# Reordering the down stage of a seven-product FFN unit in a two-layer decoder kernel

## The chip, the core and the metric

The kernel is one program on one core of a Trainium2 chip. Times are device microseconds (us) from the first to the last work of the core; the number compared is the median over several executions. The profile is of one execution, taken by the hardware profiler. TensorE multiplies matrices, VectorE (DVE) and ScalarE (ACT) work elementwise, GpSimd (POOL) does small things, SyncE (SP) issues the weight loads. PE in the rows is TensorE, PEld its weight load.

## The reference, cut to what matters

Two layers; each is an attention and pooling part, then a gated FFN with a causal three-tap convolution, then a gated per-layer embedding. The change lies in the FFN and in the stage behind it.

```python
D_MODEL = 2048; SEQ = 256; DEPTH = 2; D_FF = 5632; PLE_DIM = 256

def conv_gated_ffn(x, w_up, conv_w, conv_b, w_down):
    gu = x @ w_up                                   # (256, 2048) @ (2048, 11264)
    gate, up = gu[..., :D_FF], gu[..., D_FF:]
    gate = causal_depthwise_conv(gate, conv_w, conv_b)
    return (jax.nn.silu(gate) * up) @ w_down        # (256, 5632) @ (5632, 2048)

for i in range(DEPTH):
    ...
    h = h + conv_gated_ffn(rms_norm(h, norm_ffn_g[i]), w_up[i], conv_w[i], conv_b[i], w_down[i])
    gate = jax.nn.sigmoid(rms_norm(h, norm_ple_g[i]) @ w_ple_gate[i])
    h = h + (p[i] @ w_ple[i]) * gate
```

All of it is float32. The kernel gets that accuracy from TensorE by splitting every operand x into hi (x rounded to the fast format) and lo = x - hi, and by adding three products: hi*hi, lo*hi and hi*lo.

## The kernel before, in words

**Halves.** Weights arrive in chunks of 128 x 2048 numbers in four buffers (`raw`), loaded by SP. A chunk has two halves of 128 x 1024. ACT copies a half to `w_hi` (L989), then DVE subtracts it from the raw half into `w_lo` (L1551); I call the latter a split. There are six buffers of each kind for halves, so ACT can write half n only when TensorE has used half n-6. ACT and DVE work four halves ahead of their place in the program (`go(a, b)` splits halves a+4 to b+4-1). SP loads a chunk into a raw buffer once the last split that reads the old chunk is done (L537 to 545).

**Units.** The 5632 channels of the FFN are 11 units of 512. `first_unit` computes gate and up of unit 0. Then a loop of five rounds, two units in each, does ten times: gate (8 halves, numbers 0 to 7) and up (8 to 15) of unit u, then down of unit u-1. Behind the loop down of the last unit is done by four plain blocks (L2413). In all there are 20 loop units in the two layers.

**Down.** The product of 256 tokens x 512 channels with 512 x 2048 weights is cut by columns into four blocks of 512. Two of them are plain: two halves each, 24 matmuls per half. The other two are done together by a Strassen-like form with seven block products instead of eight: seven halves of 12 matmuls each. These are B11, B21, B22, T1, T3, T2, T4 (`corner_product`, L2341); the T weights are differences of quarters, which DVE forms in place in `raw` (`t_sum`, L1559, four subtractions of 128 x 1024). In the kernel before the seven are halves 16 to 22 and the plain blocks are halves 23 to 26, so a unit has 27 halves.

**Results.** A product lands in a PSUM bank: `acc` is two pairs of banks, `tps` four banks. DVE adds it to `h` (`by_token`, L1520) or to one of four kept sums in `corner_sum` (L1680), and the add frees the bank: it counts up `acc_free[0]`, `acc_free[1]` or `t_done`. TensorE waits for that count before it writes the bank again (`free_acc`, L1908, `new_job`, L1933). Gate of the next unit starts in `acc[0]`, so its first matmul waits for the last add out of `acc[0]`. The kept sums are combined once per layer, in `fold` (L1748), before the last unit's block is added to `h`.

**Order.** Each engine's order of work is written out by hand. There is no scheduler; an engine waits at its next instruction until its counts are there. What stands in which order on DVE in the down stage is L1714 to 1741.

Of the kernel before, what the change touches and what calls it, by code (L numbers as in the profile page):

```python
# [27 lines left out]
P = 128  # L28
# [99 lines left out]
def build(nc, x, p, positions, norm_mix_g, w_in, pool_w, pool_scale, q_norm_g, w_uq, kv_norm_g, w_ukv,  # L128
# [56 lines left out]
    with ExitStack() as ctx:  # L185
# [25 lines left out]
        with ExitStack() as early:  # L211
            sb("below_corners", [P, KT // 2, S], scope=early)
            corner_sum = sb("corner_sum", [P, 4, BLK], scope=early)
# [5 lines left out]
        mask = sb("mask", [P, 2 * P])  # L219
        win = sb("win", [P, 2, 2, PAD + S])  # L220
# [46 lines left out]
        with ExitStack() as scope:  # L267
# [4 lines left out]
            sb("below_p", [P, 3, S], scope=scope)  # L272
# [97 lines left out]

        LAT_Q, LAT_KV = 0, LKT
# [25 lines left out]
        def chunk_of(m):  # L397
# [3 lines left out]
        FORM_B11, FORM_B21, FORM_B22, FORM_T1, FORM_T3, FORM_T2, FORM_T4 = range(2 * 2 * (KT // 4), 2 * 2 * (KT // 4) + CORNERS)  # L401
        PLAIN = FORM_T4 + 1
        IN_RAW = {FORM_B11: (0, 0), FORM_B21: (0, 1), FORM_B22: (1, 1), FORM_T1: (0, 0), FORM_T3: (1, 0),
                  FORM_T2: (1, 1), FORM_T4: (0, 1)}

        def raw_half(n):

            down = 2 * (KT // 4)
            if n >= UNIT_HALVES:
                return UNIT_CHUNKS + (n - UNIT_HALVES) // 2, n - UNIT_HALVES & 1  # L410
            if n >= PLAIN:
                return down + 2 + (n - PLAIN) // 2, (n - PLAIN) & 1
            if n >= FORM_B11:
                return down + IN_RAW[n][0], IN_RAW[n][1]
            return n // 2, n & 1
# [19 lines left out]
        def _(sp):  # L435
            def load(l, c, pieces):
# [4 lines left out]
                if 0 <= c - (CH["ple"] - N_BLK) < 2:  # L441
                    m = 2 * RAW_SLOTS + M_DOWN - UNIT_HALVES + FORM_T4 + 1
# [48 lines left out]
            for l in range(L):  # L491
# [45 lines left out]
                def load_at(l, w, i, n, pieces):  # L537
                    slot = (c + n) % RAW_SLOTS
                    first = M_UNIT + i * UNIT_HALVES + 2 * RAW_SLOTS
                    freed = (-(UNIT_HALVES - 1 - FORM_T4),) * 2 + (-2, 0) if n < RAW_SLOTS else [2 * (n - RAW_SLOTS) + 2]  # L540
                    sp.wait_ge(lo_done, HALVES * l + LOOP_HALVES * w + first + freed[n if n < RAW_SLOTS else 0])
# [43 lines left out]
        def _(pool):  # L585
# [60 lines left out]
            for l in range(L):  # L646
# [12 lines left out]
                pool.memset(corner_sum[:, :, :], 0.0).then_inc(corners_zero, 1)  # L659
# [35 lines left out]
        def _(act):  # L695
# [88 lines left out]
            for l in range(L):  # L784
# [194 lines left out]
                def split_u(l, w, i, n):  # L979
# [6 lines left out]
                    if FORM_T1 <= n <= FORM_T4:  # L986
                        act.wait_ge(t_made, made(l, w, i, n - FORM_T1 + 1))
# [152 lines left out]
        def _(dve):  # L1140
# [18 lines left out]
            dve.memset(win[:, :, :, 0:PAD], 0.0)  # L1159
# [88 lines left out]
            for l in range(L):  # L1248
# [75 lines left out]
                def pooled(i):  # L1324
                    u = u_pool[i][:, :, PAD:PAD + S]
                    dve.memset(u_pool[i][:, :, 0:PAD], 0.0)
                    for k in range(2):
# [226 lines left out]
                def corner(i, k, half):  # L1554

                    slot = (CH["ffn"] + 4 * (KT // 4) + i * UNIT_CHUNKS + k) % RAW_SLOTS
                    return raw[:, slot, half * HALF:(half + 1) * HALF]

                def t_sum(w, i, k, dst, a, b):  # L1559

                    if k == 1:
                        c = CH["ffn"] + 4 * (KT // 4) + i * UNIT_CHUNKS + 1
# [104 lines left out]
                def unit(w, i):  # L1667
# [834 lines left out]
```

## Time and profile before

| what | value |
|---|---|
| median of 3 runs | 2183.87 us (2181.57, 2183.87, 2183.98) |
| the profiled execution: its time, its span | 2181.74 us, 2179.9 us |
| granted TensorE clock, mean | 0.998 of full |
| busy: PE, PEld, DVE, ACT, POOL | 99%, 85%, 79%, 51%, 2% of the span |
| chain that ended last | PE 92%, DVE 4%, issue 3% |
| DMA | 406.75 MB, mean 187 GB/s |

The table is read from the top: TensorE is busy nearly all the time, so the time is its work plus its few idle stretches. The other engines' shares are means over stages; what counts is whether one of them is late where TensorE waits for it. The slices of the span show TensorE at 9 tenths or more in all but the last, and VectorE at 8 tenths in the FFN.

### The profile page before, as it was taken

How to read it: one execution, taken by the hardware profiler on the slowest of the kernel's cores; microseconds unless marked ns; L12 is line 12 of the kernel's file. 1: busy time of each engine (PE TensorE's matmuls, PEld its weight loads, DVE VectorE, ACT ScalarE, POOL GpSimd, SP SyncE). 2: the span in 40 equal slices, each digit the busy share in tenths (PEclk: the TensorE clock that was granted, in tenths of full speed). 3: DMA queues.
4: the chain of work that ended last, by engine and by line, in shares of the span. 5: the costliest groups of instructions: out<-in, count | busy, mean ns of one | idle time of the engine just before them, and what ended most of it. 6: DMA issues, size and time to landing. Idle time of an engine off the chain costs nothing.

```text
span 2179.9 us, 32733 instructions
## 1 busy us (share of the span) xinstructions
PE 2149.6 (99%) x11526; PEld 1858.8 (85%) x11526; DVE 1730.0 (79%) x2213; ACT 1119.1 (51%) x1419; POOL 48.9 (2%) x112
## 2 busy tenths in 40 slices
PE   9999999999999999999999999999999999999998
PEld 8898888888888888878898988888888888888786
DVE  6797569888889888896557975789888889888964
ACT  6555545544455544545554654455554555554554
POOL 2000000000000000000000000000000000000011
PEclk9999999999999999999999999999999999999999
DMA  7745555446655446645556455555546655446462
GB/s 265 213 136 175 187 196 199 170 154 217 213 195 198 170 154 224 212 174 188 176 185 175 136 192 170 203 194 189 178 154 230 212 193 193 168 159 231 174 213 97
DMA packets 233323, 406.75 MB, mean 187 GB/s; under 512 B 14828, under 2 KB 50268, under 8 KB 233096
## 3 DMA queue, kind: packets, MB, share of 16 engines
q1 hardware_dynamic: 231976, 402.72, 54.8%
q0 software_dynamic: 512, 1.76, 0.2%
q8 instruction: 48, 0.79, 0.1%
q10 hardware_dynamic: 736, 1.07, 0.1%
q14 instruction: 51, 0.42, 0.1%
HBM read 403.42 MB, written 2.10 MB: 186 GB/s over the span
## 4 chain that ended last, share of the span: by engine, by line
PE 92%; DVE 4%; issue 3%; ACT 0%; DVEq 0%; POOL 0%; POOLq 0%; ACTq 0%
PE acc L2078 16%; PE tps L2078 16%; PE acc L1897 12%; PE acc L1899 12%; PE acc L1898 11%; PE tps L2088 8%; PE acc L2088 8%; DVE w_lo L1551 2%; PE tps L1898 2%; PE tps L1899 2%; PE tps L1897 2%; PE tps L1954 1%; PE acc L1984 1%; DVE h L1521 1%; DVE corner_sum L1680 1%
## 5 line engine op out<-in xcount | busy, mean ns | idle before, releaser
L989 ACT ACTIVATE w_hi<-raw 128x1024 fp32r<-128x1024 f32 x540 | 556.8, 1057 | 554.7 <-PE acc L2088 116.6
L1551 DVE TENSOR_TENSOR w_lo<-raw,w_hi 128x1024 fp32r<-128x1024 f32 x540 | 649.4, 1224 | 158.0 <-ACT w_hi L989 145.5
L1175 DVE TENSOR_TENSOR w_lo<-raw,w_hi 128x1024 fp32r<-128x1024 f32 (+1 forms) x288 | 342.4, 1211 | 144.4 <-ACT w_hi L715 138.7
L715 ACT ACTIVATE w_hi<-raw 128x1024 fp32r<-128x1024 f32 (+2 forms) x287 | 290.2, 1043 | 179.3 <-PE acc L1899 127.0
L2078 PE MATMUL acc<-xa,w_hi 128*128 128x512 f32 x1536 | 366.1, 391 | 0.0
L2078 PE MATMUL tps<-xa,w_hi 128*128 128x512 f32 x1536 | 361.2, 390 | 0.0
L2078 PEld LDWEIGHTS tps<-xa,w_hi 128*128 128x128 f32 x1536 | 285.5, 188 | 57.1
L2078 PEld LDWEIGHTS acc<-xa,w_hi 128*128 128x128 f32 x1536 | 283.9, 188 | 56.0 <-DVE h L1513 0.4
L1898 PE MATMUL acc<-w_hi,xb_lo 128*128 128x512 f32 x640 | 249.3, 390 | 0.0
L1897 PE MATMUL acc<-w_hi,xb_hi 128*128 128x512 f32 x560 | 220.8, 394 | 0.0
L1899 PE MATMUL acc<-w_lo,xb_hi 128*128 128x512 f32 x560 | 218.4, 390 | 0.0
L2088 PEld LDWEIGHTS acc<-xa,w_lo 128*128 128x128 f32 x1536 | 192.8, 192 | 5.1
L2088 PE MATMUL acc<-xa,w_lo 128*128 128x256 f32 x1536 | 194.3, 283 | 0.0
L2088 PEld LDWEIGHTS tps<-xa,w_lo 128*128 128x128 f32 x1536 | 190.7, 192 | 3.7
L2088 PE MATMUL tps<-xa,w_lo 128*128 128x256 f32 x1536 | 191.8, 283 | 0.0
L1898 PEld LDWEIGHTS acc<-w_hi,xb_lo 128*128 128x128 f32 x640 | 120.4, 188 | 23.9
L1899 PEld LDWEIGHTS acc<-w_lo,xb_hi 128*128 128x128 f32 x560 | 105.2, 188 | 22.0
L1897 PEld LDWEIGHTS acc<-w_hi,xb_hi 128*128 128x128 f32 x560 | 105.3, 188 | 20.7
L1897 PE MATMUL acc<-w_hi,gt_hi 128*128 128x512 f32 x240 | 95.7, 399 | 9.2 <-DVE w_lo L1551 9.2
L1567 DVE TENSOR_TENSOR raw<-raw 128x1024 f32<-128x1024 f32 x80 | 97.6, 1220 | 0.0
L1898 PE MATMUL acc<-w_hi,gt_lo 128*128 128x512 f32 x240 | 93.7, 390 | 0.0
L1899 PE MATMUL acc<-w_lo,gt_hi 128*128 128x512 f32 x240 | 93.6, 390 | 0.0
(263 smaller groups left out, 2676.3 us busy)
## 6 DMA issues: line engine op xcount, KB each, us to landing
raw<-in_w_up SPq DMA_DIRECT2D x176, 1024.0 KB, 5.0
raw<-in_w_down SPq DMA_DIRECT2D x88, 1024.0 KB, 5.0
raw<-in_w_out SPq DMA_DIRECT2D x32, 1024.0 KB, 5.0
raw<-in_w_ple_gate SPq DMA_DIRECT2D x32, 1024.0 KB, 5.0
raw<-in_w_in SPq DMA_DIRECT2D x21, 1024.0 KB, 5.4
raw<-in_w_ukv SPq DMA_DIRECT2D x8, 1024.0 KB, 5.6
raw<-in_w_in SPq DMA_DIRECT2D x8, 864.0 KB, 4.8
raw<-in_w_uq SPq DMA_DIRECT2D x6, 1024.0 KB, 5.6
```

Of the source, the lines that this page charges most:

```text
L715: copy(w_hi[:, half_of(m), 0:n], raw[:, c % RAW_SLOTS, at:at + n], ACT.Copy).then_inc(hi_done, 1)
L989: copy(w_hi[:, half_of(m), :], raw[:, c % RAW_SLOTS, half * HALF:(half + 1) * HALF], ACT.Copy).then_inc(hi_done, 1)
L1175: dve.tensor_tensor(w_lo[:, half_of(m), 0:n], raw[:, c % RAW_SLOTS, at:at + n], w_hi[:, half_of(m), 0:n].bitcast(F32), ALU.subtract).then_ ...
L1521: return dve.scalar_tensor_tensor(dst, src, rstd["ffn"][:, t:t + 1], dst, ALU.mult, ALU.add)
L1551: dve.tensor_tensor(w_lo[:, half_of(m), :], raw[:, slot, half * HALF:(half + 1) * HALF], w_hi[:, half_of(m), :].bitcast(F32), ALU.subtract ...
L1567: dve.tensor_tensor(dst, a, b, ALU.subtract).then_inc(t_made, 1)
L1680: ins = dve.tensor_tensor(dst, src, dst, ALU.add)
L1897: pe.matmul(dst, a_hi, b_hi, start=first, stop=False)
L1898: pe.matmul(dst, a_lo, b_hi, start=False, stop=False)
L1899: return pe.matmul(dst, a_hi, b_lo, start=False, stop=last)
L2078: ins = pe.matmul(dst, hi[:, k * BLK + n * P:k * BLK + (n + 1) * P], x_both[:, kt, :, :].rearrange("p a s -> p (a s)"), start=kt == 0, sto ...
L2088: ins = pe.matmul(bank(n, False)[:, S:2 * S], lo[:, k * BLK + n * P:k * BLK + (n + 1) * P], xa[0][:, kt, :], start=False, stop=False)
```

## The change

The order of the down stage is changed on all engines. Halves 16 and 17 are B11 and B21, then comes a plain block (18, 19), then B22 and T1 (20, 21), then the other plain block (22, 23), then T3, T2 and T4 (24 to 26). The plain blocks are now column blocks 0 and 1, the seven-product blocks 2 and 3. The seven products' weights come from chunks 10 and 11 of a unit instead of 8 and 9, the plain ones from 8 and 9. The banks move with it: the first plain block is in `acc[1]`, B22 and T1 in `tps` 0 and 1, the second plain block in `tps` 2 and 3, T3 in `acc[0]`, T2 and T4 in `tps` 0 and 1. The four subtractions for the T weights stand later on DVE. `fold` works at blocks 2 and 3 of the last unit. The kept sums are in `corner_3` and `corner_4`, cleared by two instructions on POOL; one clearing of `win` on DVE moves from the start into each layer.

```diff
@@ the numbers of the halves
-        FORM_B11, FORM_B21, FORM_B22, FORM_T1, FORM_T3, FORM_T2, FORM_T4 = range(2 * 2 * (KT // 4), 2 * 2 * (KT // 4) + CORNERS)
-        PLAIN = FORM_T4 + 1
+        DOWN = 4 * (KT // 4)
+        FORM_B11, FORM_B21, PLAIN_0, _, FORM_B22, FORM_T1, PLAIN_1, _, FORM_T3, FORM_T2, FORM_T4 = range(
+            DOWN, DOWN + N_BLK + CORNERS)
...
+        LAST_LO = (PLAIN_0 + 1, PLAIN_1 + 1, FORM_T4, FORM_T4)
@@ loads, SP
-                    freed = (-(UNIT_HALVES - 1 - FORM_T4),) * 2 + (-2, 0) if n < RAW_SLOTS else [2 * (n - RAW_SLOTS) + 2]
+                    if n < RAW_SLOTS:
+                        freed = max(LAST_LO[n] + 1 - UNIT_HALVES, 2 * (n + 1) - 2 * RAW_SLOTS)
+                    else:
+                        freed = 2 * (n - RAW_SLOTS) + 2
@@ one unit, DVE
                     tap_1(u)
                     go(12, 13)
                     tap_0(u)
+                    go(13, 15)
+                    silu(u)
+                    go(15, 16)
                     t_sum(w, i, 1, corner(i, 0, 0), corner(i, 1, 0), corner(i, 0, 0))
-                    go(13, 15)
+                    go(16, 17)
                     t_sum(w, i, 2, corner(i, 1, 0), corner(i, 1, 1), corner(i, 1, 0))
-                    silu(u)
+                    gated(u)
+                    go(17, 18)
                     t_sum(w, i, 3, corner(i, 1, 1), corner(i, 1, 1), corner(i, 0, 0))
-                    go(15, 16)
+                    go(18, 20)
+                    dve.wait_ge(corners_zero, 2 * l + 2)
+                    product_added(FORM_B11, sum_p1, acc[0][:, 0, :], None, acc_free[0])
+                    product_added(FORM_B21, h_block(0, 2), acc[0][:, 1, :], 0, acc_free[0])
                     t_sum(w, i, 4, corner(i, 0, 1), corner(i, 0, 1), corner(i, 1, 1))
-                    go(16, 17)
-                    gated(u)
-                    go(17, 19)
-                    dve.wait_ge(corners_zero, l + 1)
-                    product_added(FORM_B11, corner_sum[:, 0], acc[0][:, 0, :], None, acc_free[0])
-                    product_added(FORM_B21, h_block(0, 0), acc[0][:, 1, :], 0, acc_free[0])
-                    go(19, 21)
-                    product_added(FORM_B22, h_block(0, 1), acc[1][:, 0, :], 0, acc_free[1])
-                    product_added(FORM_T1, corner_sum[:, 1], acc[1][:, 1, :], None, acc_free[1], 3)
-                    go(21, 22)
-                    product_added(FORM_T3, corner_sum[:, 2], tps[:, 0, :], None, t_done)
-                    product_added(FORM_T2, corner_sum[:, 3], tps[:, 1, :], None, t_done)
-                    go(22, 23)
-                    product_added(FORM_T4, h_block(1, 0), tps[:, 2, :], 1, t_done)
-                    go(23, 25)
-                    for t in range(TT):
-                        product_added(PLAIN + 1, h_block(t, 2), acc[0][:, t, :], t, acc_free[0])
-                    go(25, 27)
-                    for t in range(TT):
-                        product_added(PLAIN + 3, h_block(t, 3), tps[:, (3 + t) % T_BANKS, :], t, t_done, 1 if t == 0 else 4)
+                    go(20, 22)
+                    product_added(PLAIN_0 + 1, h_block(0, 0), acc[1][:, 0, :], 0, acc_free[1])
+                    product_added(PLAIN_0 + 1, h_block(1, 0), acc[1][:, 1, :], 1, acc_free[1], 3)
+                    go(22, 24)
+                    product_added(FORM_B22, h_block(0, 3), tps[:, 0, :], 0, t_done)
+                    product_added(FORM_T1, sum_p5, tps[:, 1, :], None, t_done)
+                    go(24, 26)
+                    product_added(PLAIN_1 + 1, h_block(0, 1), tps[:, 2, :], 0, t_done)
+                    product_added(PLAIN_1 + 1, h_block(1, 1), tps[:, 3, :], 1, t_done)
+                    product_added(FORM_T3, sum_p7, acc[0][:, 0, :], None, acc_free[0], 2)
+                    go(26, 27)
+                    product_added(FORM_T2, sum_p6, tps[:, 0, :], None, t_done)
+                    product_added(FORM_T4, h_block(1, 2), tps[:, 1, :], 1, t_done, 3)
@@ the last unit, DVE (fold)
-                    if j >= 2:
+                    if j < 2:
                         return
@@ one unit, TensorE
                     corner_product(m0 + FORM_B11, w, a11, acc[0][:, 0, :])
                     corner_product(m0 + FORM_B21, w, a12, acc[0][:, 1, :])
+                    for _ in down(m0 + PLAIN_0, b0 + 3, gt, w):
+                        pass
                     pe.wait_ge(s_split_lo, (UNITS - 1) * l + u)
-                    free_acc(l, b0 + 3, w)
-                    corner_product(m0 + FORM_B22, w, s4, acc[1][:, 0, :])
-                    corner_product(m0 + FORM_T1, w, s1, acc[1][:, 1, :])
-                    for n, a in ((0, s3), (1, s2), (2, a22)):
-                        corner_product(m0 + FORM_T3 + n, w, a, new_job(l, j0 + 4 + n, w))
-                    for _ in down(m0 + PLAIN, b0 + 4, gt, w):
+                    corner_product(m0 + FORM_B22, w, s4, new_job(l, j0 + 4, w))
+                    corner_product(m0 + FORM_T1, w, s1, new_job(l, j0 + 5, w))
+                    for _ in down(m0 + PLAIN_1, None, gt, w, j0 + 6):
                         pass
-                    for _ in down(m0 + PLAIN + 2, None, gt, w, j0 + 7):
-                        pass
+                    free_acc(l, b0 + 4, w)
+                    corner_product(m0 + FORM_T3, w, s3, acc[0][:, 0, :])
+                    corner_product(m0 + FORM_T2, w, s2, new_job(l, j0 + 8, w))
+                    corner_product(m0 + FORM_T4, w, a22, new_job(l, j0 + 9, w))
```

The end of a unit on DVE before, from the add of T4 on (`w_lo` rows are splits, rows with `rstds` add a product to `h`):

```order
L1521 SCALAR_TENSOR_TENSOR h<-tps,rstds,h 128x512 [waits w_used]
L1551 TENSOR_TENSOR w_lo<-raw,w_hi 128x1024 [waits w_used,hi_done] x2
L395 REGISTER_ALU
L1521 SCALAR_TENSOR_TENSOR h<-acc0,rstds,h 128x512 [waits w_used] x2
L1549 REGISTER_ALU
L1551 TENSOR_TENSOR w_lo<-raw,w_hi 128x1024 [waits w_used,hi_done] x2
L395 REGISTER_ALU
L1521 SCALAR_TENSOR_TENSOR h<-tps,rstds,h 128x512 [waits w_used] x2
```

The same end on DVE in the changed kernel, from the splits of halves 28 and 29 on:

```order
L1556 REGISTER_ALU
L1558 TENSOR_TENSOR w_lo<-raw,w_hi 128x1024 [waits w_used,hi_done]
L1556 REGISTER_ALU
L1558 TENSOR_TENSOR w_lo<-raw,w_hi 128x1024 [waits w_used,hi_done]
L1528 SCALAR_TENSOR_TENSOR h<-tps,rstds,h 128x512 [waits w_used] x2
L396 REGISTER_ALU
L1687 TENSOR_TENSOR corner_3<-acc0,corner_3 128x512 [waits w_used]
L1558 TENSOR_TENSOR w_lo<-raw,w_hi 128x1024 [waits w_used,hi_done]
L396 REGISTER_ALU
L1687 TENSOR_TENSOR corner_3<-tps,corner_3 128x512 [waits w_used]
L396 REGISTER_ALU
L1528 SCALAR_TENSOR_TENSOR h<-tps,rstds,h 128x512 [waits w_used]
```

Before, the last adds out of `acc0` had two splits and two adds behind them. Now the last add out of `acc0` (T3) has one split and two adds behind it, and two splits and two adds of the second plain block directly ahead.

DVE between the last tap of the convolution and the silu before, with the first two subtractions for the T weights (`raw<-raw`):

```order
L1567 TENSOR_TENSOR raw<-raw 128x1024 [waits raw_landed3]
L1549 REGISTER_ALU
L1551 TENSOR_TENSOR w_lo<-raw,w_hi 128x1024 [waits w_used,hi_done]
L1549 REGISTER_ALU
L1551 TENSOR_TENSOR w_lo<-raw,w_hi 128x1024 [waits w_used,hi_done]
L1566 REGISTER_ALU
L1567 TENSOR_TENSOR raw<-raw 128x1024 [waits t_made]
L1616 REGISTER_ALU
L1617 SCALAR_TENSOR_TENSOR conv<-gate_f,conv 128x1024 [waits tanh_done]
```

The same place in the changed kernel:

```order
L1556 REGISTER_ALU
L1558 TENSOR_TENSOR w_lo<-raw,w_hi 128x1024 [waits w_used,hi_done]
L1556 REGISTER_ALU
L1558 TENSOR_TENSOR w_lo<-raw,w_hi 128x1024 [waits w_used,hi_done]
L1623 REGISTER_ALU
L1624 SCALAR_TENSOR_TENSOR conv<-gate_f,conv 128x1024 [waits tanh_done]
L1556 REGISTER_ALU
L1558 TENSOR_TENSOR w_lo<-raw,w_hi 128x1024 [waits w_used,hi_done]
L1570 ISA
L1574 TENSOR_TENSOR raw<-raw 128x1024 [waits raw_landed1]
```

The first subtraction stood directly behind the last tap; now three splits and the silu stand between them.

TensorE at the end of a unit in the changed kernel, T4 and the first matmuls of the next gate:

```order
L1903 MATMUL tps<-w_hi,gt_hi 128x512 [waits lo_done]
L1904 MATMUL tps<-w_hi,gt_lo 128x512
L1905 MATMUL tps<-w_lo,gt_hi 128x512
L1903 MATMUL tps<-w_hi,gt_hi 128x512
L1904 MATMUL tps<-w_hi,gt_lo 128x512
L1905 MATMUL tps<-w_lo,gt_hi 128x512
L1911 REGISTER_ALU
L1919 REGISTER_ALU [waits lo_done]
L2084 MATMUL acc0<-xa,w_hi 128x512 [waits acc_free0]
```

The wait for `acc_free0` ahead of the gate was there before too; what stands ahead of it is now T4 in `tps` and not a plain block.

## Rows read from the trace of the kernel before

**Rows 1.** One loop unit: length, busy time of each engine, PEclk, DMA share, GB/s

```profile
635.10:700.70 65.60, 65.14 (x349) 56.22 (x348) 57.00 (x67) 32.52 (x33) 0.00 (x0) 1.00 0.56 192
```

**Rows 2.** Waits of TensorE, whole span: waiter, releaser: us in total, times, longest

```profile
PE acc L1897 <- DVE w_lo L1551: 9.2, 20, 0.5
PE tps L1954 <- DVEq L1518: 8.6, 4, 2.6
...
PE tps L1954 <- DVE h L1521: 1.2, 2, 0.6
```

**Rows 3.** Timeline of TensorE in that unit: start, us, instruction [idle before, releaser]

```profile
631.35 0.84 PE L2078 MATMUL acc<-xa,w_hi 128*128 128x512 f32 x3
...
675.81 0.39 PE L1897 MATMUL acc<-w_hi,gt_hi 128*128 128x512 f32 x1
...
685.10 0.39 PE L1899 MATMUL tps<-w_lo,gt_hi 128*128 128x512 f32 x1
685.95 0.49 PE L1897 MATMUL acc<-w_hi,gt_hi 128*128 128x512 f32 x1 [0.46 <-DVE w_lo L1551]
...
696.95 3.79 PE L2078 MATMUL acc<-xa,w_hi 128*128 128x512 f32 x16
```

**Rows 4.** Timeline of DVE in the same unit, second half

```profile
667.31 1.22 DVE L1567 TENSOR_TENSOR raw<-raw 128x1024 f32<-128x1024 f32 x1
669.47 2.36 DVE L1551 TENSOR_TENSOR w_lo<-raw,w_hi 128x1024 fp32r<-128x1024 f32 x2 [0.94 <-ACT w_hi L989]
...
681.07 2.35 DVE L1551 TENSOR_TENSOR w_lo<-raw,w_hi 128x1024 fp32r<-128x1024 f32 x2
683.34 0.69 DVE L1680 TENSOR_TENSOR corner_sum<-acc,corner_sum 128x512 f32<-128x512 f32 x1
683.94 0.74 DVE L1521 SCALAR_TENSOR_TENSOR h<-acc,rstds,h 128x512 f32<-128x512 f32 x1
...
694.52 1.41 DVE L1521 SCALAR_TENSOR_TENSOR h<-acc,rstds,h 128x512 f32<-128x512 f32 x2
...
699.43 2.36 DVE L1551 TENSOR_TENSOR w_lo<-raw,w_hi 128x1024 fp32r<-128x1024 f32 x2
```

**Rows 5.** Timeline of ACT in the same unit

```profile
663.08 1.07 ACT L989 ACTIVATE w_hi<-raw 128x1024 fp32r<-128x1024 f32 x1 [2.70 <-PE tps L2078]
...
668.40 3.10 ACT L989 ACTIVATE w_hi<-raw 128x1024 fp32r<-128x1024 f32 x3
674.19 1.07 ACT L989 ACTIVATE w_hi<-raw 128x1024 fp32r<-128x1024 f32 x1 [2.70 <-PE tps L2078]
```

**Rows 6.** The loads of chunks 10 and 11, and all loads' time to landing

```profile
657.92 5.80 SPq L544 DMA_DIRECT2D raw<-in_w_down  x2
...
DMA to landing us min/median/max: 4.8/5.0/7.1
```

**Rows 7.** Timeline of TensorE behind the last unit of layer 0

```profile
979.95 1.09 PE L1954 MATMUL tps<-ident,h 128*128 128x128 f32 x8 [2.62 <-DVEq L1518]
986.36 1.09 PE L1954 MATMUL tps<-ident,h 128*128 128x128 f32 x8
...
996.37 0.48 PE L1897 MATMUL acc<-w_hi,xb_hi 128*128 128x512 f32 x1
```

**Rows 8.** ACT there: the copies that free the banks of the embedding product

```profile
994.94 2.03 ACT L1065 ACTIVATE pw<-acc 128x512 f32<-128x512 f32 x4
```

**Rows 9.** POOL and DVE at the start of the last unit's down, layer 0

```profile
956.77 2.51 POOL L662 TENSOR_TENSOR xa<-conv,xa 128x1024 fp32r<-128x1024 f32 x1 [672.60 <-ACT xa L1042]
...
958.25 3.24 DVE L1551 TENSOR_TENSOR w_lo<-raw,w_hi 128x1024 fp32r<-128x1024 f32 x2
```

**Rows 10.** The same place in layer 1: TensorE, and the granted clock

```profile
2060.64 1.97 PE L1954 MATMUL tps<-ident,h 128*128 128x128 f32 x8 [2.62 <-DVEq L1518]
...
2068.47 1.03 PE L1954 MATMUL tps<-ident,h 128*128 128x128 f32 x8
...
2060.00:2062.00 2.00, 1.36 (x7) 1.36 (x8) 1.75 (x2) 1.38 (x5) 0.00 (x0) 0.55 0.47 180
```

More of the change, by code:

```diff
@@ L219, in build @@
         mask = sb("mask", [P, 2 * P])
+        with ExitStack() as early:
+            corner_3 = sb("corner_3", [P, 3, BLK], scope=early)
         win = sb("win", [P, 2, 2, PAD + S])
@@ L369, in build @@
         t_made = sem("t_made")
+        sum_p1, sum_p7, sum_p6, sum_p5 = corner_3[:, 0], corner_3[:, 1], corner_3[:, 2], corner_4[:, :]
         LAT_Q, LAT_KV = 0, LKT
@@ L399, in chunk_of @@
             return m // 2 if m < M_DOWN else (m - EXTRA) // 2
[L401 to L404 removed]
+        DOWN = 4 * (KT // 4)
+        FORM_B11, FORM_B21, PLAIN_0, _, FORM_B22, FORM_T1, PLAIN_1, _, FORM_T3, FORM_T2, FORM_T4 = range(
+            DOWN, DOWN + N_BLK + CORNERS)
+        IN_RAW = {PLAIN_0: (0, 0), PLAIN_0 + 1: (0, 1), PLAIN_1: (1, 0), PLAIN_1 + 1: (1, 1),
+                  FORM_B11: (2, 0), FORM_B21: (2, 1), FORM_B22: (3, 1), FORM_T1: (2, 0), FORM_T3: (3, 0),
+                  FORM_T2: (3, 1), FORM_T4: (2, 1)}
+        T_ORDER = (FORM_T1, FORM_T3, FORM_T2, FORM_T4)
+        LAST_LO = (PLAIN_0 + 1, PLAIN_1 + 1, FORM_T4, FORM_T4)
         def raw_half(n):
[L408 removed]
             if n >= UNIT_HALVES:
                 return UNIT_CHUNKS + (n - UNIT_HALVES) // 2, n - UNIT_HALVES & 1
[L411 to L414, printed above, removed]
+            if n >= DOWN:
+                return 2 * (KT // 4) + IN_RAW[n][0], IN_RAW[n][1]
             return n // 2, n & 1
@@ L658, in _ @@
                     p_landed, 16)
-                pool.memset(corner_sum[:, :, :], 0.0).then_inc(corners_zero, 1)
+                pool.memset(corner_3[:, :, :], 0.0).then_inc(corners_zero, 1)
+                pool.memset(corner_4[:, :], 0.0).then_inc(corners_zero, 1)
                 pool.wait_ge(g_hi, UNITS * l + UNITS)
@@ L1157, in _ @@
             step(dve.reciprocal(inv_cnt[:, :], inv_cnt[:, :]))
-            dve.memset(win[:, :, :, 0:PAD], 0.0)
             step(dve.memset(k_lo[ROPE:P, 0, :].bitcast(F32), 0.0))
@@ L1326, in pooled @@
                     dve.memset(u_pool[i][:, :, 0:PAD], 0.0)
+                    if i == 0:
+                        dve.memset(win[:, :, :, 0:PAD], 0.0)
                     for k in range(2):
@@ L1748, in fold @@
                 def fold(l, j):
-                    if j >= 2:
+                    if j < 2:
                         return
-                    p1, p5, p7, p6 = (corner_sum[:, k] for k in range(4))
-                    if j == 0:
+                    p1, p5, p7, p6 = sum_p1, sum_p5, sum_p7, sum_p6
+                    if j == 2:
                         dve.wait_ge(acc_free[0], BLOCKS * l + BL["ple"] - N_BLK + 2)
-                        dve.wait_ge(acc_free[1], BLOCKS * l + BL["ple"] - N_BLK)
                         dve.wait_ge(t_done, JOBS * l + JB["p"] + T_BANKS)
-                    done = 8 * l + 4 * j
-                    if j == 0:
+                    done = 8 * l + 4 * (j - 2)
+                    if j == 2:
                         dve.tensor_tensor(p6, p6, p1, ALU.add).then_inc(corner_folded, 1)
-                        by_token(h[:, 0, 0:BLK], p1, 0).then_inc(corner_folded, 1)
+                        by_token(h[:, 0, 2 * BLK:3 * BLK], p1, 0).then_inc(corner_folded, 1)
                         dve.wait_ge(corner_folded, done + 2)
```

26 lines of the change are left out of this document (12 added, 14 removed).

## The prediction

> **What bounds the kernel now.** I read four views in this order: busy time by stretch, waits of TensorE, timelines of one loop unit engine by engine, and the stage behind the last unit. The stretch of one loop unit shows a length of 65.60 us with TensorE busy for 65.14 and DVE for 57.00 [rows 1]. So TensorE sets the length and DVE has 8.6 us to spare, but as a mean over the unit. The waits say where DVE is late all the same: 20 times, once per loop unit, TensorE waits 0.46 us for a split; behind the last unit of a layer it waits for `h` (two waits of 2.62 us, so 1.7 for each of the other two, and two of 0.6) [rows 2].
>
> I count unit time from the first gate matmul at 631.35. The down stage starts at 675.81, which is 44.46. 41 matmuls later, at 685.10, one sees the pace, 9.29 / 41 = 0.2266 us [rows 3]. So a short half (12 matmuls) takes 2.72 / 2 = 1.36 us and a plain half (24) 5.44 / 2 = 2.72 us. All 90 matmuls take 20.40, while the stage took 696.95 - 675.81 = 21.14: the lost time is 0.74 us per unit, around the wait at 685.95 [rows 3]. Twenty of those, 14.8 us, is all that a better order of the down stage could win.
>
> DVE: the splits at 681.07 (two, the next instruction at 683.34) give 1.135 us for an instruction on 128 x 1024; the add at 683.34 gives 0.60 for an add to a kept sum, and two adds in 1.41 us, of which one takes 0.74, give 0.66 for an add to `h` [rows 4]. From 669.47 (unit time 38.12) until the next unit's first splits at 699.43 the DVE rows follow one another with no idle time: 29.96 us, which is 14 splits, three subtractions and the silu (18 x 1.135), 2.5 for the two steps of the gated product, four adds to kept sums and seven to `h`. That stretch is the tight place. Its last instructions run 2.5 us into the next unit, which costs nothing today, because the last add out of `acc[0]` starts at 694.52 and is over at 695.93, a microsecond before the next gate needs that bank at 696.95 [rows 3, 4].
>
> **The change, part by part.** *Order on TensorE.* The same 90 matmuls, so 20.40 us. Start of each half in unit time without waits: B11 44.46, B21 45.82, plain 47.18 and 49.90, B22 52.62, T1 53.98, plain 55.34 and 58.06, T3 60.78, T2 62.14, T4 63.50, end 64.86. The next gate could start at 64.86.
>
> *Splits.* In the new order of DVE, half 23 is split after 17 to 22, the silu, the gated product and three subtractions: 38.12 + 11 x 1.135 + 2.5 = 53.1, against a need at 58.06. Half 26 has, beyond that, one subtraction, three splits and four adds: 53.1 + 4 x 1.135 + 0.60 + 3 x 0.66 = 60.2, against 63.50. So the wait of today goes: -0.74.
>
> *What is late next: the add of T3.* T3 is in `acc[0]`, the bank where the next gate starts, and its add stands on DVE behind the splits of 28 and 29 and both adds of the second plain block. I get its place by difference. The first subtraction moves out of the time before 38.12 into the stretch, so the stretch has 29.96 + 1.135 = 31.10 us. Behind T3's add stand one split, T2's add and T4's: 1.135 + 0.60 + 0.66 = 2.40. T3's add therefore ends (with the 0.09 by which rows overlap) at 38.12 + 28.70 + 0.09 = 66.91. One small idle time comes in: half 20's hi copy ends at 674.19 + 1.07, unit time 43.91 [rows 5], and DVE would be free for its split at 38.12 + 5 x 1.135 = 43.80: 0.11 more. TensorE starts 0.13 after DVE's end (split over at 683.34 + 0.60 + 0.66 + 1.22 = 685.82, matmul at 685.95). The next gate starts at 66.91 + 0.11 + 0.13 = 67.15, not at 64.86: a wait of 2.3 us in place of one of 0.74, so +1.55 us on 65.60.
>
> Does DVE come back into step? It would be done with the unit at 66.9 + 0.1 + 2.3 = 69.3, which is 2.2 us into the next unit (2.5 today), and its splits in the gate stage wait for TensorE's pace as before, so the stretch again starts at 38.12. The start is set by ACT: its copies of halves 17 to 19 start at 668.40 behind the tanh, and the first ends at 669.47 [rows 5]. The subtraction that stands at 667.31 today fills that time; now DVE idles there. Each unit hence takes 67.15. The bank of T2 needs B22's add, due at about 62.3 against 62.14: 0.2 us, swallowed by the longer wait. Twenty times the stage hands over to something that starts in `acc[0]` (18 gates, and twice the last unit's blocks): 20 x 1.55 = +31.0. Bounds: if the idle time of 0.11 doesn't come, 20 x 1.44 = 28.8; if DVE lost one more row of 0.4 us to a hi copy that comes late, 20 x 1.95 = 39. I take 31.0.
>
> *Loads.* Halves 16 and 17 now come from chunk 10, which is issued at 657.92 and lands in 5.0 us at the median, 662.9; ACT wants it at 663.08 [rows 5, 6]. Cost 0, by 0.2 us of margin; at the longest landing seen, 7.1, it would be 1.9 late, of which DVE, still in its taps then, hides about 0.4. Chunk 11 is wanted 10 us after it lands, and the next gate's first two chunks are issued earlier than today: 0.
>
> *Behind the last unit.* Folds at blocks 0 and 1 are gone: the waits of 1.7 and 2.6 fall away, and so does the 0.6 (T2's add is over by 68.7, TensorE wants its bank at 67.15 + 2.72). With no fold TensorE runs from one transposition to the next without a wait, 979.95 to 986.36 [rows 7]. The fold at block 2 brings a wait of 2.6 back. The one at block 3 is hidden from the transpositions, but it delays ACT's copies that free the embedding product's banks: today the first two are over at 994.94 + 1.0, and TensorE starts in that bank at 996.37 [rows 7, 8], so of 2.7 us of fold 2.3 come out as a wait. Removed 4.9, added 4.9 per layer: 0, between -2.3 (if the copies aren't what waits) and +0.4.
>
> *POOL at the last unit.* Its subtraction takes 2.51 us, and beside it two splits took 3.24 instead of 2.36 [rows 9]. In the new order ACT frees it at about 64.4, so it ends at about 67.0, just when TensorE may start: 0 to 1.0 per layer; I take 0.5, +1.0 in all. The Trainium skill, page "SBUF — State Buffer", section "SBUF: two separate sides", has an exclusive lock there between GpSimd and a VectorE instruction with two SBUF inputs; the rows agree in that one side is held up, and by the lock POOL would start only after the split of 29, some 0.6 later.
>
> *The rest.* Clearing the sums in two pieces is hidden in POOL's 98% of idle time; the clearing of `win` stands where DVE waits for ACT; 0.
>
> Sum: 31.0 + 0 + 1.0 = +32.0 on the profiled execution's 2181.74 (its span and 1.8 us around it): 2213.7. Two of the three runs shown stand 2.2 us above it, so the median would be nearer 2216; I say 2215.
>
> **The rivals.** *A. The clock falls in the new waits.* In layer 1 a wait of 2.62 us was followed by a granted clock of 0.55 over two microseconds, a mix of 2.4 GHz and 1.2 GHz, and the way to the next transpositions took 2068.47 - 2060.64 = 7.83 us against 6.41 in layer 0 after the same wait, which did not lower it [rows 7, 10]: 1.4 us. The new wait of 2.3 lies between that and the waits of 1.7, after which nothing fell. If it fell after half of them: 2215 + 14 = 2229, after all of them 2243. Against: the full clock in layer 0, and the work before and after is dense. The Trainium skill, page "TensorE: Matmul & The Clock Gate", section "A second HAM failure mode: psum-queue depth-cycling", says that frequent short idles between groups of matmuls let the clock go to and fro; by that rule the time is this rival's. The trace agrees only in part, since 20 waits of 0.46 left the clock at full.
>
> *B. Faster: DVE catches up, and the new order pays.* T3's add would have to end by 64.86 - 0.13 = 64.7, which is 2.3 us, two splits, earlier. It would, if DVE's stretch began right behind the last tap at 667.31 (35.96) instead of waiting for ACT until 38.12, or if instructions were shorter in their new places. Then the 0.74 is won 20 times: 2167. Against: the wait for the hi copy behind the tanh is in every unit, and no row of the stretch has any idle time to give.
>
> *C. The add is late by only 0.6 to 0.9 us* (some of the work counted is done elsewhere); gain and loss cancel, 2182. Nothing in the rows speaks for it.
>
> *D. Chunk 10 lands late* in most units, DVE's stretch begins 1.5 us later: 20 x 1.5 = +30, 2245. For it: the margin of 0.2 us. Against: the load is alone on its queue, and the median landing is 5.0.
>
> **How the numbers follow.** Forecast 66%, A 22%, D 5%, B 4%, C 3%. The forecast's own range is 2208 to 2224, by the bounds of 28.8 and 39, the two levels of the runs, -4.6 to +0.8 behind the last units and 0 to 2 for POOL. To leave out no more than 2 in 10 I go up to A at half of the waits: 2206 to 2232. A measurement of this kernel tells a change from none at about 0.2%, 4.4 us. Slower by more than that: 66 + 22 + 5 = 93%; within: 3%; faster: 4%.
>
> **What would show it.** Loop units of 67.15 us; a wait of about 2.3 us ahead of each gate, put down to the add of `corner_3` out of `acc`, 18 times, and twice ahead of the last unit's first block; no more wait for a split in the down stage; an idle time of 2.1 us on DVE between the last tap and the next split; behind the last units no wait at the first two transpositions, one of 2.6 at the third and one of 2.3 at the embedding gate; a full clock in the loop. I am wrong if the units are under 65.6 us, if the wait has another releaser, or if the clock is below full in them.

## The result and the profile after

The changed kernel takes 2216.46 us (median of 4 runs, 2214.65 to 2218.10), the kernel before 2182.72 (4 runs, 2181.55 to 2183.98): a ratio of 1.0154, 95% interval 1.0137 to 1.0172. The forecast was 2215. The profiled execution took 2217.96 with a span of 2216.2. It lies at the high end of its runs and the profiled execution before (2181.74) at the low end of its own, so the two spans differ by 36.3 us where the medians differ by 33.7.

One loop unit in the changed kernel, in the columns of [rows 1]; the stretch is 0.24 us shorter than the unit:

```profile
641.00:708.00 67.00, 65.20 (x346) 55.92 (x345) 56.94 (x67) 32.12 (x34) 0.00 (x0) 1.00 0.53 186
```

TensorE is busy for as long as before and the clock is full, so the longer unit is waiting. The first waits of TensorE over the whole span, longest in total first, to be held against [rows 2]:

```profile
PE acc L2084 <- DVE corner L1687: 30.6, 18, 1.7
PE acc L1903 <- DVE h L1528: 5.1, 2, 2.6
PE tps L1960 <- DVEq L1525: 4.6, 2, 2.3
PE acc L1903 <- POOL xa L668: 4.0, 2, 2.0
```

The 20 waits for a split are gone. In their place stand 18 waits ahead of a gate, for an add out of `acc` to a kept sum. TensorE at that place, answering to [rows 3]:

```profile
639.77 1.43 PE L2084 MATMUL acc<-xa,w_hi 128*128 128x512 f32 x5 [1.70 <-DVE corner L1687]
...
684.35 0.39 PE L1903 MATMUL acc<-w_hi,gt_hi 128*128 128x512 f32 x1
...
702.30 0.49 PE L1903 MATMUL tps<-w_hi,xb_lo 128*128 128x512 f32 x1
...
707.00 0.72 PE L2084 MATMUL acc<-xa,w_hi 128*128 128x512 f32 x2 [1.70 <-DVE corner L1687]
```

From gate to gate 707.00 - 639.77 = 67.23 us; the other units of layer 0 that begin behind such a wait take 67.23 to 67.29, and I use 67.24 below. The row at 702.30 is the start of T2. It has no wait in brackets, yet it starts 0.49 after the start of the matmul ahead of it where 0.23 is the pace, and the next one is 0.09 late too: 0.35 lost. DVE in the same unit, answering to [rows 4]:

```profile
674.28 1.66 DVE L1618 SCALAR_TENSOR_TENSOR conv<-gate_f,prm_all,conv 128x254 f32<-128x254 f32 x4
678.01 2.36 DVE L1558 TENSOR_TENSOR w_lo<-raw,w_hi 128x1024 fp32r<-128x1024 f32 x2 [2.08 <-ACT w_hi L995]
...
682.56 1.22 DVE L1574 TENSOR_TENSOR raw<-raw 128x1024 f32<-128x1024 f32 x1
683.84 1.23 DVE L1558 TENSOR_TENSOR w_lo<-raw,w_hi 128x1024 fp32r<-128x1024 f32 x1
...
701.41 0.75 DVE L1528 SCALAR_TENSOR_TENSOR h<-tps,rstds,h 128x512 f32<-128x512 f32 x1
702.08 0.69 DVE L1687 TENSOR_TENSOR corner<-tps,corner 128x512 f32<-128x512 f32 x1
702.67 2.36 DVE L1558 TENSOR_TENSOR w_lo<-raw,w_hi 128x1024 fp32r<-128x1024 f32 x2
704.94 1.41 DVE L1528 SCALAR_TENSOR_TENSOR h<-tps,rstds,h 128x512 f32<-128x512 f32 x2
706.26 0.69 DVE L1687 TENSOR_TENSOR corner<-acc,corner 128x512 f32<-128x512 f32 x1
```

The idle time of 2.08 behind the last tap is there. From 678.01 on DVE has two small gaps, one ahead of 683.84 (0.14 later than the pace of its rows gives) and one of 0.15 in the gated product; T3's add (706.26) ends at 706.95 and the gate starts 0.05 later. B22's add (701.41) ends at 702.16, and T2, which needs its bank, starts at 702.30.

Behind the last unit of layer 0, the transpositions (`ident`) and the two waits that aren't theirs; of before see [rows 7]:

```profile
976.29 0.50 PE L1903 MATMUL acc<-w_hi,xa 128*128 128x512 f32 x1 [2.02 <-POOL xa L668]
...
985.06 1.03 PE L1960 MATMUL tps<-ident,h 128*128 128x128 f32 x8
991.39 1.04 PE L1960 MATMUL tps<-ident,h 128*128 128x128 f32 x8
1000.22 1.09 PE L1960 MATMUL tps<-ident,h 128*128 128x128 f32 x8 [2.30 <-DVEq L1525]
1009.35 0.50 PE L1903 MATMUL acc<-w_hi,ppt_hi 128*128 128x512 f32 x1 [2.56 <-DVE h L1528]
```

Four microseconds there, with the granted clock in the column before the last two:

```profile
1008.00:1012.00 4.00, 2.65 (x8) 2.07 (x9) 2.52 (x3) 2.62 (x6) 0.89 (x5) 0.75 0.43 167
```

The 0.75 is a mean: behind the wait of 2.56 a part of these four microseconds ran at full clock (2.4 GHz) and a part at half (1.2 GHz). Stretches like it come in three places of the changed kernel between 300 and 2150 us (from 1008, 2072 and 2108), in one of the kernel before (2060), and never in the loop.

Where the 36.3 us between the two spans are, by the starts of the loop's first gate and of the last unit's first block in each layer: the ten units of layer 0 16.59 and those of layer 1 16.60, 1.3 from there to the loop of layer 1, 1.4 behind the start of layer 1's last unit, 0.3 ahead of the first gate.

### The profile page after: what moved, and what is told of

Same layout as the page of the kernel before. It is cut to its first block, busy times and chain, and to the rows that moved or that the text cites. A ratio compares the mean times of both kernels' runs of the same rounds, so it can differ in the third digit from the quotient of the medians.

```text
span 2216.2 us, 32786 instructions
## 1 busy us (share of the span) xinstructions
PE 2158.6 (97%) x11526; PEld 1859.3 (84%) x11526; DVE 1731.8 (78%) x2214; ACT 1120.8 (51%) x1419; POOL 49.8 (2%) x114
## 4 chain that ended last, share of the span: by engine, by line
issue 63%; PE 34%; DVE 2%; POOL 1%; ACT 1%; POOLq 0%; DVEq 0%; ACTq 0%
PE acc L1903 8%; PE acc L1905 8%; PE acc L1904 8%; PE acc L2084 3%; PE acc L2094 1%; PE tps L2084 1%; PE tps L1960 1%; PE acc L1990 1%; PE tps L2094 1%; DVE h L1528 1%; DVE xb_lo L1192 0%; POOL xa L668 0%; PE tps L1904 0%; PE tps L1905 0%; PE tps L2259 0%
## 5 line engine op out<-in xcount | busy, mean ns | idle before, releaser
L2084 PE MATMUL acc<-xa,w_hi 128*128 128x512 f32 x1536 | 368.7, 392 | 30.6 <-DVE corner L1687 30.6
L1904 PE MATMUL acc<-w_hi,xb_lo 128*128 128x512 f32 x600 | 233.4, 389 | 0.0
L1904 PEld LDWEIGHTS acc<-w_hi,xb_lo 128*128 128x128 f32 x600 | 112.8, 188 | 22.5
```

The lines of the kernel that those rows point to most:

```text
L1904: pe.matmul(dst, a_lo, b_hi, start=False, stop=False)
L2084: ins = pe.matmul(dst, hi[:, k * BLK + n * P:k * BLK + (n + 1) * P], x_both[:, kt, :, :].rearrange("p a s -> p (a s)"), start=kt == 0, sto ...
```

## The experiments

The first two edits and that of the first subtraction are made to the changed kernel; of the others the text says to which kernel of this section. The kernel before ran beside each of them on the same chip: 2183.58 us (19 runs) beside the first four, 2183.37 (9 runs) beside the last three, and 2182.72 beside the changed kernel. The ratios are to these; a difference to the changed kernel or between the two groups is across chips, and good to about a microsecond. The theories A, B and C of this section are those of each run's own expectation, not the rivals A to D of the prediction.

**T3's add earlier.**

```diff
-                    go(24, 26)
+                    go(24, 25)
+                    product_added(FORM_T3, sum_p7, acc[0][:, 0, :], None, acc_free[0], 2)
+                    go(25, 26)
                     product_added(PLAIN_1 + 1, h_block(0, 1), tps[:, 2, :], 0, t_done)
                     product_added(PLAIN_1 + 1, h_block(1, 1), tps[:, 3, :], 1, t_done)
-                    product_added(FORM_T3, sum_p7, acc[0][:, 0, :], None, acc_free[0], 2)
```

> Only the add of T3 moves on DVE: it stands behind the split of half 28, ahead of the split of 29 and the two adds of the second plain block. Theory A (the next gate waits for the bank that T3's add frees, by that add's place in DVE's order): the add ends 1.135 + 1.32 = 2.46 us earlier, at 64.8 of unit time, so the gate starts when TensorE is through, at 64.9, plus 0.2 for T2's bank, which then shows: units of 65.1 us instead of 67.24. The last unit of each layer still waits for POOL's subtraction (it ends at about 67.1), so 18 x 2.15 = 38.7 us less than the changed kernel: about 2178. Theory B (DVE's work in the down stage as a whole is the bound, and whatever TensorE needs next waits for its end): nothing is removed from DVE, the wait goes to another instruction, units of 67.2, about 2216.

2180.49 us (10 runs), 0.9987 of before, interval 0.9977 to 0.9997, and 2.5 above A's number. The whole loss is in the place of this one add; theory B is out. TensorE's waits and a unit of that kernel:

```profile
PE tps L1961 <- DVEq L1525: 4.6, 2, 2.3
PE acc L1904 <- POOL xa L668: 2.9, 2, 1.5
PE tps L1961 <- DVE corner L1687: 2.4, 2, 1.2
PE acc L1904 <- DVE h L1528: 2.1, 2, 1.1
```

```profile
629.97 3.79 PE L2085 MATMUL acc<-xa,w_hi 128*128 128x512 f32 x16
...
692.36 0.49 PE L1904 MATMUL tps<-w_hi,xb_lo 128*128 128x512 f32 x1
...
695.22 3.79 PE L2085 MATMUL acc<-xa,w_hi 128*128 128x512 f32 x16
```

No gate waits any more, and still the unit is 65.25 and not 64.86. What is left is the row at 692.36: T2 starts late by the same 0.35 as in the changed kernel. Under a gate that waited anyway this cost nothing; with that wait gone it is what sets the unit.

**T3's add later**: behind the split of half 30 instead of ahead of it.

```diff
-                    product_added(FORM_T3, sum_p7, acc[0][:, 0, :], None, acc_free[0], 2)
                     go(26, 27)
+                    product_added(FORM_T3, sum_p7, acc[0][:, 0, :], None, acc_free[0], 2)
```

> Only the add of T3 moves, the other way: behind the split of half 30, one instruction of 1.135 us later. A: units of 67.24 + 1.135 = 68.4 us, 20 x 1.135 = 22.7 us more than the changed kernel, about 2239. B: DVE's work is the same, so the time is that of the changed kernel, about 2216.

2256.0 us (4 runs), ratio 1.0325 (1.0308 to 1.0343): A's direction, and 17 us more than A's number; theory B is out. The profile is of the slowest of the four (2263.84, the others 2252.31 to 2258.25). The gate waits 2.8 instead of 1.7, as A has it. The rest shows in three gates of that kernel and in the four microseconds of the last two:

```profile
371.52 6.73 PE L2084 MATMUL acc<-xa,w_hi 128*128 128x512 f32 x16 [2.82 <-DVE corner L1687]
...
650.93 5.38 PE L2084 MATMUL acc<-xa,w_hi 128*128 128x512 f32 x16 [2.83 <-DVE corner L1687]
...
720.75 3.94 PE L2084 MATMUL acc<-xa,w_hi 128*128 128x512 f32 x16 [2.82 <-DVE corner L1687]
```

```profile
648.00:652.00 4.00, 1.17 (x4) 0.88 (x4) 4.00 (x6) 2.95 (x3) 0.00 (x0) 0.83 1.05 410
720.00:724.00 4.00, 3.25 (x14) 2.70 (x15) 4.00 (x6) 1.24 (x2) 0.00 (x0) 1.00 1.05 406
```

The same 16 matmuls behind the same wait take 5.38 us in one unit and 3.94 in the other, and the clock is below full in the first alone: 1.44 a time. At the gate of 371.52 the clock was down for longer (0.50 as the mean of 372 to 376), and they take 6.73. In this execution 12 of the 18 gates are slow ones and six are not; in both layers it is every third gate that is spared. The span is 45.8 us longer than the changed kernel's. 18 gates with 1.13 more and two first blocks of a last unit with 1.8 more (3.8 instead of 2.0) make 23.9. The other 21.9 are close to 15 times 1.44, by the count of the falls: 12 gates and both first blocks, two of these 14 falls twice as long, less one, since two more falls come behind the last units where the changed kernel has three. That is rival A of the prediction, at waits of 2.8. Behind the 1.7 of the change it didn't come in one of 18.

**The first subtraction back** behind the last tap, where it stood before.

```diff
                     tap_0(u)
+                    t_sum(w, i, 1, corner(i, 0, 0), corner(i, 1, 0), corner(i, 0, 0))
                     go(13, 15)
                     silu(u)
                     go(15, 16)
-                    t_sum(w, i, 1, corner(i, 0, 0), corner(i, 1, 0), corner(i, 0, 0))
                     go(16, 17)
```

> Only the first of the four subtractions for the T weights goes back to where it stood, right behind the last tap, into the 2.1 us in which DVE now idles. A and B both: DVE's stretch is 1.135 us shorter, so T3's add ends 1.135 earlier, units of 66.1 us; 18 x 1.135 = 20.4 us less than the changed kernel (the last unit of a layer is held by POOL), about 2196. A third theory C (the idle time on DVE is none that can be filled, since the chunk that the subtraction reads lands at 36.9 of unit time and pushes the stretch back) expects 2205 or more.

2216.89 us (4 runs), ratio 1.0154: nothing, against 20 us that A and B both expected. DVE in that kernel, where the gate of this unit starts at 639.35:

```profile
676.47 1.22 DVE L1574 TENSOR_TENSOR raw<-raw 128x1024 f32<-128x1024 f32 x1 [0.95 <-DMA raw<-in_w_down]
677.62 2.35 DVE L1558 TENSOR_TENSOR w_lo<-raw,w_hi 128x1024 fp32r<-128x1024 f32 x2
...
683.42 1.23 DVE L1558 TENSOR_TENSOR w_lo<-raw,w_hi 128x1024 fp32r<-128x1024 f32 x1 [1.18 <-ACT w_hi L995]
```

The subtraction fills part of the idle time, and the same time is lost at the split of half 20, whose hi copy ends at the same moment of the unit as in the changed kernel (44.03 of unit time in both), because ACT copies it only when TensorE is done with an earlier half. Theory C named a time that fits (2205 or more), but not by its mechanism: the subtraction does wait 0.95 for its chunk, yet the splits behind it start at 38.27 of the unit, where the changed kernel has 38.24, so nothing is pushed back. So DVE's stretch is tied down twice: at the hi copy behind the tanh, and again at half 20. Work that is moved ahead of the first tie alone gains nothing.

**Both edits together**, T3's add earlier and the first subtraction back, by the two diffs above:

> T3's add early (as in the first) and the first subtraction back (as in the second). A: T3's add is over at 63.7 and B22's at 61.2 of unit time, so neither bank is waited for; units are TensorE's 90 matmuls and the gate and up stage, 64.9 us; 18 x 2.35 = 42 us less than the changed kernel, about 2174, which is below the kernel before (2183). B: 2196, as in the second.

2180.37 us (10 runs), ratio 0.9989 (0.998 to 0.9999). As the add's edit alone, and missing A and B alike: a unit is 65.23, and T2 still starts late by 0.35, since B22's add hangs on the stretch behind half 20.

**Two subtractions moved**: to the kernel with the first subtraction back, the second ahead of the split of half 20.


```diff
                     go(15, 16)
-                    go(16, 17)
                     t_sum(w, i, 2, corner(i, 1, 0), corner(i, 1, 1), corner(i, 1, 0))
+                    go(16, 17)
```

> The change with both the first subtraction put back right behind the last tap and the second moved ahead of the split of half 20. Theory A (DVE's stretch is anchored a second time, at the split of half 20, whose hi copy waits for TensorE's half 14; work moved ahead of that anchor fills the idle time there): T3's add comes 1.13 us earlier, units 66.1 instead of 67.24, so 18 x 1.135 = 20.4 less, 2196. Theory B (the end of the unit isn't set by DVE's work behind half 20): 2216 as with the first subtraction alone.

2208.44 us (4 runs), ratio 1.012 (1.0105 to 1.0136): 8 us less than the changed kernel where A had 20. DVE there:

```profile
674.35 1.22 DVE L1574 TENSOR_TENSOR raw<-raw 128x1024 f32<-128x1024 f32 x1 [0.90 <-DMA raw<-in_w_down]
...
681.35 1.23 DVE L1558 TENSOR_TENSOR w_lo<-raw,w_hi 128x1024 fp32r<-128x1024 f32 x1
683.13 1.23 DVE L1629 TENSOR_TENSOR up_f<-tps,up_f 128x1024 f32<-128x1024 f32 x1 [0.55 <-ACT up_f L1039]
```

The split of half 20 no longer waits, as A has it. A third tie then holds: the gated product waits 0.55 for ACT's copy of what TensorE has just finished. Its gate rows at 570.53 and 704.02, two units apart, give a unit of 66.75, which is 0.49 less, and 18 x 0.49 = 8.8. Theory A's mechanism holds, its size doesn't.

**B22's add early too**, in the kernel with T3's add earlier.

```diff
-                    go(22, 24)
+                    go(22, 23)
                     product_added(FORM_B22, h_block(0, 3), tps[:, 0, :], 0, t_done)
+                    go(23, 24)
```

> The first of these experiments (T3's add behind the split of half 28), and with it B22's add, which frees the T bank that T2 uses, ahead of the split of half 27 instead of behind it. Theory A (T2 still starts 0.36 us late in each unit because B22's add ends only then): the hiccup goes, a unit is 64.87 us instead of 65.24, so 18 x 0.37 = 6.6 less than 2180.5, 2174, faster than before by 0.45%. Theory B (the hiccup has another cause, or the splits that are now later hold TensorE up instead): unit 65.24, 2180.5.

2175.18 us (5 runs), ratio 0.9965 (0.9951 to 0.9978). A unit and TensorE's waits:

```profile
627.75 3.83 PE L2086 MATMUL acc<-xa,w_hi 128*128 128x512 f32 x16
...
692.65 3.83 PE L2086 MATMUL acc<-xa,w_hi 128*128 128x512 f32 x16
```

```profile
PE acc L1905 <- DVE h L1528: 5.1, 2, 2.6
PE acc L1905 <- POOL xa L668: 4.8, 2, 3.0
PE tps L1962 <- DVEq L1525: 4.6, 2, 2.3
```

64.90 us with no gap in the down stage, as A says: T2's late start was its bank. The loop has given back 0.70 of the 0.74 us per unit that the prediction named as all there is to win. 20 units x 0.70 = 14.0, and the span is only 6.5 shorter than before's. The rest went behind the last units: 4.8 for POOL, waited for 1.8 and 3.0 us there, and the clock fell in three places behind the last units (from 952, 988 and 2032) instead of one (2 x 1.4).

**The stage behind the last unit too**, in the kernel with both adds early. The first plain half starts with the products of the activations' hi part and waits for POOL's lo part only then; T2's add stands ahead of the split of half 30; the fold is spread; the last block is added before the kept sums.

```diff
-                pe.wait_ge(g_lo, UNITS * l + UNITS)
+                pe.wait_ge(g_hi, UNITS * l + UNITS)
...
+                    pe.wait_ge(g_lo, UNITS * l + UNITS)
@@ one unit, DVE
-                    go(26, 27)
                     product_added(FORM_T2, sum_p6, tps[:, 0, :], None, t_done)
+                    go(26, 27)
@@ last unit, DVE
-                    fold(l, j)
-                    add_block(l, bd + j, j)
...
+                    if j < N_BLK - 1:
+                        add_block(l, bd + j, j)
+                    else:
+                        last_block(bd + j)
...
+                    if j < 3:
+                        (fold_a, fold_b, fold_c)[j]()
```

> All of the experiment with B22's add early, and behind the last unit of a layer: the first plain half there begins with the products that need only the activations' hi part, so that POOL's lo part has 1.8 us more; T2's add stands ahead of the split of half 30; the fold of the kept sums is spread over blocks 0, 1 and 2, and the last block is added from its bank before the kept sums are added to h. Theory A (each of these waits is a delay of the end): per layer 1.4 (POOL), 1.2 (p transposition), about 1.8 of the 2.30 and about 1 ahead of the embedding product, 5.4 x 2 = 11 with the falls of the clock behind them some 1 to 4 more: 2174 - 11 = 2163, down to 2160. Theory B (the waits only move to the next transposition or to the embedding gate): 2172 to 2175.

2163.17 us (5 runs, 2162.96 to 2165.20), ratio 0.9912 (0.9898 to 0.9925): faster than both kernels, at A's number. Its waits, and the p transposition of layer 0:

```profile
...
PE acc L1920 <- ACT pw L1071: 2.0, 2, 1.0
PE tps L1977 <- DVE corner L1687: 1.9, 1, 1.9
PE acc L2456 <- POOL xa L668: 1.1, 1, 1.1
```

```profile
957.28 0.63 PE L1977 MATMUL tps<-ident,p_tok 128*128 128x128 f32 x4 [1.88 <-DVE corner L1687]
```

The folds no longer hold up a transposition: the 4.9 us of waits per layer that stood behind the last unit before, and moved with the change, are gone. What stands there instead is one wait for T2's add (behind the split that POOL holds up), one for POOL, and two for ACT's copies for the embedding gate. Not all of the 4.9 is won by that. From the start of the last unit's first block to the loop of layer 1 this kernel takes as long as the kernel before (424.5 and 424.7 us), since the wait of 1.88, one of 0.99 and a fall of the clock took the place of the folds' waits; behind the start of that block in layer 1 it takes 135.8 against 139.9. The four edits were made at once, so the run doesn't say what each is worth: of the 12.1 us by which the span is shorter than with both adds early, some 5 lie ahead of the last units' first blocks, where POOL was waited for, and some 7 behind.

## Why the prediction was right

*The order on TensorE, and what could be won.* Forecast 64.86 us for a unit without waits, 0.74 to win. Measured 64.90 once nothing waited. One count in the text is off by two and cancels: the trace has 6 matmuls in a half of the seven products and 12 in a plain half (T2's six start at 702.30 to 703.55), not 12 and 24; the 90 per unit and the times of 1.36 and 2.72 are right.

*The add of T3 as the next thing late.* Right in place, mechanism and size: the add takes away the gate's bank, the unit is 67.24 against 67.15 forecast, +1.64 against +1.55, so 20 x 1.64 = 32.8 us, and 16.59 + 16.60 = 33.2 by the starts. Taking that add alone to an earlier place gives the loss back, and to a later one lengthens the wait by 1.13. The forecast wait of 2.3 shows as 1.70, as the trace counts it; the time lost against 64.90 is 2.34. 0.35 of it is T2's late start, which the prediction put at 0.2. Some 0.3 more is in no listed wait: a wait is counted from the end of the last matmul's row, 0.39 behind its start, where the next would have started after 0.23 (0.16), and the matmul behind the wait's end has its successor 0.1 late. A reader who multiplies the listed waits by their number gets 30.6 us where 18 x 2.34 = 42.1 were lost against a unit that never waits; the unit's length is the number to take. Before, the listed 0.46 stood for 0.74 in the same manner.

*DVE back in step at each unit.* Right: its stretch began at unit time 38.24 (38.12 forecast). The idle time that the prediction gave to the wait for half 20 (0.11) is there, as 0.14. What it didn't see is that this small gap is a second tie, which makes the first one worthless to remove. That touched no term of the sum, but it misled the expectation for the first subtraction by 20 us, and would mislead an engineer about the remedy. Nor is it so that no row of the stretch has idle time: before the change too, the second step of the gated product waits 0.15.

*Loads, nothing.* Right: in a unit nothing waits for chunks 8 to 11. ACT does wait for gate and up chunks, 15 times and 2.4 us at the longest (before, 36 times and 5.1), but no wait of TensorE hangs on it. The waits of 0.95, 1.01 and 0.90 in the three experiments with the first subtraction moved show that the margin was thin for a reader earlier than ACT.

*Behind the last units, nothing in sum.* Right for the waits, 4.86 listed per layer against 4.9 before, but 2.7 us were lost there (1.3 and 1.4). Their size is that of the clock's falls: one more in each layer than before, at about 1.4 each. The prediction looked for a fall at the gates (rival A) and put none here. Its reason for the waits is partly wrong too. 2.30 stands at the third transposition (2.6 forecast). The wait of 2.3 that was to stand at the embedding gate, by ACT's copies, is one of 2.56 at the embedding product whose bank holds block 3, and its releaser is DVE's add to `h`. The step that failed is "hidden from the transpositions, but it delays ACT's copies": it delays first the add that frees the bank. In the experiment that adds the last block ahead of the kept sums this wait is gone, and ACT's copies are waited for, by 1.0 a layer.

*POOL.* Forecast 1.0 in all, as what it costs beyond DVE's add. POOL's subtraction in the last unit of layer 0 of the changed kernel, and the split beside POOL's in the kernel with T3's add earlier:

```profile
973.31 2.92 POOL L668 TENSOR_TENSOR xa<-conv,xa 128x1024 fp32r<-128x1024 f32 x1 [688.78 <-ACT xa L1048]
```

```profile
955.47 3.36 DVE L1558 TENSOR_TENSOR w_lo<-raw,w_hi 128x1024 fp32r<-128x1024 f32 x1
```

POOL ends at 976.23, and TensorE starts at 976.29; T3's add was over at 975.93, and a gate starts 0.05 behind that add, so TensorE's own bank would have let it go some 0.3 us earlier. That is the term that was to be 0.5 per layer; the listed 2.02 is mostly the gate's wait in another place. In the other kernel POOL's subtraction runs from 955.38 to 957.75, and the split that starts at 955.47 takes 3.36 us instead of 1.22. That is close to the one standing still while the other runs: 2.28 of POOL's are left when it starts, and 1.22 are its own, 3.50 if nothing overlapped. In the changed kernel DVE came first and POOL's took 2.92 instead of 2.37, 0.55 more where the prediction names 0.6. The Trainium skill, page "SBUF — State Buffer", section "SBUF: two separate sides", has an exclusive lock there, and the trace agrees to within 0.2 us.

*The rivals.* A didn't come: the loop's clock is full behind all 18 waits of 1.70. It was no idle worry, since one split more in front of the add brought it at 12 of the 18 gates. The Trainium skill, page "TensorE: Matmul & The Clock Gate", section "A second HAM failure mode: psum-queue depth-cycling", warns of frequent short idles between groups of matmuls; frequent idles of 1.7 did nothing here, frequent ones of 2.8 did. B needed the add two splits earlier; one split and two adds were enough for the gate, and its 2167 wasn't reached by that alone (2180), nor with T2's bank (2175), for the waits behind the last units. C and D: no row speaks for them.

*The sum.* Gates and units 32.8 (31.0 forecast), POOL 0.6 (1.0), behind the last units 2.7 (0), ahead of the loop 0.3 (0): 36 us between the profiled executions where 32.0 was forecast. By the medians the change costs 33.7, and the forecast is 1.4 short; by the profiled executions it is 4.3 short. The falls of the clock that it leaves out are in the profiled execution; how many the other runs had isn't on record, so how much of the closeness is luck stays open.

## What to carry to other kernels

When a kernel's order is changed to take away a wait, count, for each bank that TensorE comes back to, when the add that frees it ends, by its place in the other engine's queue; the wait moves to the latest of them. Here three adds stood one to three instructions too late (T3's, B22's, T2's), and the same change that cost 1.5% gained 0.9% with them moved, the folds spread and TensorE's first products behind the last unit taken from what was ready. An idle time on a busy engine isn't worth its length: look for the next tie behind it (here a copy that follows TensorE's pace, and behind that another) before you move work into it.

## What the runs showed of the hardware

A wait that the trace lists as w costs about w + 0.3 on TensorE in this kernel (0.46 cost 0.74, and 1.70 cost 1.99), and a late start of 0.35 (T2's) appears with no wait beside it at all; only the distance between the starts of successive matmuls shows it.

The clock fell behind some waits and not behind others of the same length: behind none of the 18 of 1.70 in the changed kernel's loop and none of the 18 of 1.7 with the first subtraction back, behind 12 of the 18 of 2.8 and both of 3.8 with T3's add later, and in both outcomes for 2.62 (layer 0 and layer 1 of before, [rows 7, 10]). The changed kernel has both outcomes for the same instruction behind the same wait, at the last unit's first block of layer 0 (976.29, above) and of layer 1:

```profile
976.00:980.00 4.00, 3.71 (x18) 3.12 (x19) 3.71 (x4) 0.22 (x1) 0.23 (x1) 1.00 1.01 390
...
2074.86 0.72 PE L1903 MATMUL acc<-w_hi,xa 128*128 128x512 f32 x1 [2.00 <-POOL xa L668]
...
2076.00:2080.00 4.00, 4.00 (x17) 3.16 (x16) 2.28 (x3) 0.06 (x1) 0.00 (x0) 0.70 1.01 388
```

The shortest waits at which it fell were 1.82 (both adds early) and 1.88, the latter in the kernel with the stage behind the last unit changed:

```profile
956.00:960.00 4.00, 2.72 (x10) 2.26 (x11) 4.00 (x6) 2.06 (x3) 0.00 (x0) 0.74 0.47 154
```

In all nine traces, from 300 us to the last block, each fall stands at a listed wait of 1.82 or more, and none stands at the some 60 waits of 1.2 to 1.71. Between 1.8 and 2.9 both outcomes occur, so the length of one wait doesn't decide it; what does stays open. A fall cost 1.4 us where it could be read from two like stretches, and 1.4 to 1.6 by the lengths of the units with T3's add later (69.8 to 70.0 against 68.4; 71.2 behind the long one).
